# Attention on TensorE in steps of two heads instead of one, on one core of a two-block model

## What is computed

```
z = einsum('bhqd,bhkd->bhqk', qb, k) * scale            # qb: a block of 128 queries
# stick-breaking:
log_keep = where(past, log_sigmoid(-z), 0.0)
log_later = cumsum(log_keep, axis=3, reverse=True) - log_keep
w = where(past, exp(log_sigmoid(z) + log_later), 0.0)
o = einsum('bhqk,bhkd->bhqd', w, v)
# softmax (latent heads of 64 + 32 columns):
s = where(kpos <= qpos, z, neg);  p = softmax(s);  o = einsum('bhqk,bhkd->bhqd', p, v)
```

## Time and profile before

| | |
|---|---|
| median of 3 runs | 2439.66 us (2438.17 to 2441.11) |
| the profiled execution's own time | 2441.37 us |
| its span, first to last instruction | 2439.6 us |
| PE busy | 2364.3 us (97%) |
| DVE busy | 1379.0 us (57%) |
| ACT busy | 980.8 us (40%) |
| POOL busy | 241.9 us (10%) |

### The profile page before, as it was taken

One profiled execution on the slowest core, in us unless ns is written; L12 is line 12 of the kernel. 1 busy time (PEld: TensorE's weight loads), 2 busy tenths in 40 slices (PEclk: granted clock), 3 DMA queues, 4 the chain that ended last, 5 costly groups with the idle time before them and its releaser, 6 DMA issues.

```text
span 2439.6 us, 35763 instructions
## 1 busy us (share of the span) xinstructions
PE 2364.3 (97%) x13448; PEld 1887.9 (77%) x13448; DVE 1379.0 (57%) x1936; ACT 980.8 (40%) x1507; POOL 241.9 (10%) x192
## 2 busy tenths in 40 slices
PE   8999999999999999999999999999999999999998
PEld 6765777888887765777888887777888888788887
DVE  4557867666545447857656545675443445533443
ACT  5535435323235535535323244564332233422332
POOL 0041210000022032301000002101000001000001
PEclk9999999999999999999999998999999999999999
DMA  4210014656432211003656521222222232222322
GB/s 158 81 61 24 19 49 143 192 195 193 144 103 78 87 61 35 19 29 122 197 190 195 167 95 60 87 86 93 98 95 95 95 97 76 78 95 96 100 97 86
DMA packets 68796, 248.33 MB, mean 102 GB/s; under 512 B 7632, under 2 KB 8144, under 8 KB 68688
## 3 DMA queue, kind: packets, MB, share of 16 engines
q1 hardware_dynamic: 68688, 246.85, 30.8%
HBM read 244.72 MB, written 2.10 MB: 101 GB/s over the span
## 4 chain that ended last, share of the span: by engine, by line
PE 85%; DVE 7%; ACT 4%; issue 2%; DMA 0%; POOL 0%; SPq 0%; DVEq 0%; ACTq 0%
PE dense L588 24%; PE dense L590 24%; PE dense L589 24%; PE aux L695 2%; PE aux L882 1%; ACT wh L1352 1%; PE aux L852 1%; DVE wl L1966 1%; PE aux L869 1%; PE aux L960 1%; PE aux L971 1%; PE aux L1056 1%; PE aux L856 1%; PE dense L616 1%; PE aux L702 0%
## 5 line engine op out<-in xcount | busy, mean ns | idle before, releaser
L588 PE MATMUL dense<-xh,wh 128*128 128x512 f32 x1840 | 734.0, 399 | 25.4 <-DVE wl L1966 10.7
L1352 ACT ACTIVATE wh<-raw 128x1024 fp32r<-128x1024 f32 x346 | 366.7, 1060 | 944.0 <-PE dense L590 936.8
L1966 DVE TENSOR_TENSOR wl<-raw,wh 128x1024 fp32r<-128x1024 f32 x346 | 427.1, 1235 | 535.4 <-ACT wh L1352 533.9
L590 PE MATMUL dense<-xh,wl 128*128 128x512 f32 x1840 | 718.3, 390 | 0.0
L589 PE MATMUL dense<-xl,wh 128*128 128x512 f32 x1840 | 718.2, 390 | 0.0
L588 PEld LDWEIGHTS dense<-xh,wh 128*128 128x128 f32 x1840 | 346.6, 188 | 122.2 <-issue 28.0
L590 PEld LDWEIGHTS dense<-xh,wl 128*128 128x128 f32 x1840 | 346.4, 188 | 73.5
L589 PEld LDWEIGHTS dense<-xl,wh 128*128 128x128 f32 x1840 | 346.7, 188 | 73.0 <-issue 4.1
L588 PE MATMUL dense<-hidh,wh 128*128 128x512 f32 x928 | 363.5, 392 | 4.9 <-DVE hidl L1998 2.1
L589 PE MATMUL dense<-hidl,wh 128*128 128x512 f32 x928 | 361.9, 390 | 0.0
L590 PE MATMUL dense<-hidh,wl 128*128 128x512 f32 x928 | 361.7, 390 | 0.0
(11 more groups left out here) (386 smaller groups left out, 2432.6 us busy)
## 6 DMA issues: line engine op xcount, KB each, us to landing
raw<-stream SPq DMA_DIRECT2D x362, 512.0 KB, 3.4
mraw<-mod_stream SPq DMA_DIRECT2D x96, 512.0 KB, 4.2
x<-x_t SPq DMA_DIRECT2D x4, 512.0 KB, 7.2
y_t<-x SPq DMA_DIRECT2D x8, 256.0 KB, 2.0
cst<-consts SPq DMA_DIRECT2D x1, 993.0 KB, 9.3
band<-bands SPq DMA_DIRECT2D x1, 576.0 KB, 4.6
cond<-c_rows SPq DMA_DIRECT2D x1, 512.0 KB, 10.5
pv_next<-vecs SPq DMA_DIRECT2D x3, 82.5 KB, 4.6
```

Source lines behind the costliest of these rows:

```text
L588: pe.matmul(o, a, h, start=first, stop=False)
L590: return pe.matmul(o, b, h, start=False, stop=last)
L1352: act.activation(wh[:, slot].rearrange("p k m -> p (k m)"), raw[:, slot, :], ACT.Copy).then_inc(hi_done, 1)
L1966: tt(wl[:, slot].rearrange("p k m -> p (k m)"), raw[:, slot, :], wh[:, slot].rearrange("p k m -> p (k m)").bitcast(F32), SUB)\
```

## The change

PE's attention goes in 16 steps j of two units, 2j and 2j+1. A step is now: dense part of unit 2j; scores of both heads of step j+1, their two large matmuls next to each other and then the two masks; turn of unit 2j; values of step j-1, for each block of keys first head 0, then head 1; turn of unit 2j+1; dense part of unit 2j+1. `bonus` and `key_norm` follow the turn of their unit. The turned weights get a third place, and ACT's copy of unit u waits for the values of unit u-3. The order on DVE and ACT stays.

```diff
+        wT_slots = (wT[:, 0, :], wT[:, 1, :], at("wT_third", [P, S], wag_at + 2048)[:])
...
-                def scores(u):
-                    kind, pair, i, e = UNITS[u]
-                    n, q0, z = (i + 1) * P, i * P, zbank[u % 3]
-                    if u >= 3:
-                        pe.wait_ge(w_act, L * NU + u - 2)
...
+                def scores(j):
+
+                    kind, pair, i, _ = UNITS[2 * j]
+                    n, q0 = (i + 1) * P, i * P
+                    z = [zbank[(2 * j + e) % 3] for e in range(2)]
+                    if j >= 1:
+                        pe.wait_ge(w_act, L * NU + 2 * j - 1)
+                    for e in range(2):
+                        if kind == "sb":
+                            r = slice(64 * e, 64 * e + 64)
+                            pe.matmul(z[e][:, 0:n], sbq[r, pair, q0:q0 + P], sbk[r, pair, 0:n],
+                                      start=True, stop=False)
...
+                    for e in range(2):
+                        pe.matmul(z[e][:, q0:q0 + P], top_half(const("ident")), top_half(neg),
+                                  start=False, stop=True)\
+                          .then_inc(z_ready, 1)
...
-                def values(u):
-                    kind, pair, i, e = UNITS[u]
+                def values(j):
+                    kind, pair, i, _ = UNITS[2 * j]
                     q = (2 if kind == "mla" else 0) + pair
-                    pe.wait_ge(wT_ready, L * NU + u + 1)
-                    if i == 0 and e == 0 and q >= 2:
+                    pe.wait_ge(wT_ready, L * NU + 2 * j + 2)
+                    if i == 0 and q >= 2:
...
+                    for k in range(i + 1):
+                        for e in range(2):
+                            m = pe.matmul(aux[4 + q % 2][64 * e:64 * e + 64, i * P:(i + 1) * P],
+                                          v[:, k, 128 * pair + 64 * e:128 * pair + 64 * e + 64],
+                                          wT_slots[(2 * j + e) % 3][:, k * P:(k + 1) * P],
+                                          start=(k == 0), stop=(k == i), skip_group_check=True)
+                    m.then_inc(av_done, 2)
...
-                scores(1)
-                for u in range(NU):
+                for j in range(NU // 2):
+                    u = 2 * j
                     if u < SB_UNITS:
                         krv_part(u)
-                    if u == 0:
+                    if j == 0:
                         pe.wait_ge(lora_read, L * 12 + 12)
-                    if u + 2 < NU:
-                        scores(u + 2)
+                    if j + 1 < NU // 2:
+                        scores(j + 1)
                     turn(u)
-                    if u >= 1:
-                        values(u - 1)
...
-                values(NU - 1)
+                    others(u)
+                    if j >= 1:
+                        values(j - 1)
+                    turn(u + 1)
+                    others(u + 1)
+                    if u < SB_UNITS:
+                        krv_part(u + 1)
+                values(NU // 2 - 1)
...
-                    if u >= 2:
-                        act.wait_ge(av_done, L * NU + u - 1)
-                    act.activation(wT[:, u % 2, 0:n], aux[2][:, 0:n], ACT.Copy)\
+                    if u >= 3:
+                        act.wait_ge(av_done, L * NU + (u - 3) // 2 * 2 + 2)
+                    act.activation(wT_slots[u % 3][:, 0:n], aux[2][:, 0:n], ACT.Copy)\
                        .then_inc(wT_ready, 1)
```

More of the change, by code:

```diff
@@ L844, in attention @@
             def attention(L, pl):
-                def scores(u):
-                    kind, pair, i, e = UNITS[u]
-                    n, q0, z = (i + 1) * P, i * P, zbank[u % 3]
-                    if u >= 3:
-                        pe.wait_ge(w_act, L * NU + u - 2)
[L850 to L857, removed]
+                def scores(j):
[9 more added lines that the diff above has]
+                                      start=True, stop=False)
+                        else:
+                            h = 2 * pair + e
+                            pe.matmul(z[e][:, 0:n], qh[0:96, h, q0:q0 + P], kh[0:96, h, 0:n],
+                                      start=True, stop=False)
                     neg = const("neg_sb" if kind == "sb" else "neg_mla")
-                    pe.matmul(z[:, q0:q0 + P], top_half(const("ident")), top_half(neg),
-                              start=False, stop=True)\
-                      .then_inc(z_ready, 1)
+                    for e in range(2):
+                        pe.matmul(z[e][:, q0:q0 + P], top_half(const("ident")), top_half(neg),
+                                  start=False, stop=True)\
+                          .then_inc(z_ready, 1)
                 def turn(u):
@@ L918, in attention, with others @@
                 pe.wait_ge(up_act, L * 6 + 6)
-                scores(0)
-                scores(1)
-                for u in range(NU):
-                    if u < SB_UNITS:
-                        krv_part(u)
-                    if u == 0:
-                        pe.wait_ge(lora_read, L * 12 + 12)
-                    if u + 2 < NU:
-                        scores(u + 2)
-                    turn(u)
-                    if u >= 1:
-                        values(u - 1)
+                def others(u):
                     if u in BONUS_AT:
@@ L934, in attention @@
                         key_norm(KEYS_AT.index(u))
-                values(NU - 1)
+                scores(0)
+                for j in range(NU // 2):
+                    u = 2 * j
+                    if u < SB_UNITS:
+                        krv_part(u)
+                    if j == 0:
+                        pe.wait_ge(lora_read, L * 12 + 12)
+                    if j + 1 < NU // 2:
+                        scores(j + 1)
+                    turn(u)
+                    others(u)
[3 more added lines that the diff above has]
+                    others(u + 1)
+                    if u < SB_UNITS:
+                        krv_part(u + 1)
+                values(NU // 2 - 1)
             def prepare_chunks(L):
```

## The result

The changed kernel takes 2447.05 us (median of 10 runs, 2444.31 to 2451.33) where the kernel before, beside it, takes 2441.48 us (10 runs, 2438.17 to 2444.99): a ratio of 1.0024, 95% interval 1.0015 to 1.0034. It is slower by 5.6 us. The forecast was 2431.9 us, with a range from 2424 to 2443, so the time lies outside the range on the slower side. The profiled execution took 2450.43 us with a span of 2448.7 us, 9.1 us more than the span before.

A forecast was written before the change was run, and what follows sets the result against it. PE was taken to bound the stick-breaking stage, with PE and DVE both near full in the softmax units. Per layer 12.1 - 9.7 = 2.4 us plus 1.5 softmax gives 3.9, 7.8 for both: 2431.9 us, range 2424 to 2443.

The forecast's parts named there:

- Both overlaps: Stick-breaking units: two heads' scores and values each run twice as fast on PE, saving 5.9 and 4.5 us a layer.
- The dense entries: Dense share of the stick-breaking stage: 16 entries on PE become 9, saving 1.5 us a layer in fixed parts.
- The waits at the second turn: Stick-breaking steps: PE waits for DVE's weights or ACT's copy, sum 9.7 us a layer, 2.55 us in step 1.
- the 12.1 us taken off PE: PE's queue before unit 16, per layer: savings in scores, values, dense entries and second turns, less turning unit 15.
- The third place for turned weights: Frees ACT's copy from the values before last; ACT is idle there, so worth nothing by itself.
- what is added: PE waits at the second turn: Stick-breaking stage: DVE's order unchanged, less PE work ahead of second turns, so 9.7 us of waits a layer, uncovered.
- the wait of 1.29 us: Ahead of unit 16, kernel before: followed by a window at clock 1.00, cited against the low clock coming earlier.
- The softmax term: Softmax units: values fall by some 5.5 us but DVE limits next, so 1.5 us gained a layer.
- the third rival: Clock stays low among the softmax units as PE idles longer: 2458 us if it covers the stretch; 8%.
- Values don't overlap: Rival: scores overlap but products with values don't, most of that overlap only turning into waiting; 2434.9 us; 12%.
- nothing overlaps: Rival: neither scores nor values overlap, 1.7 us saved, 3.3 us of waits a layer; 2442.9 us; 12%.
- The waits stay away: Rival: ACT and DVE pulled ahead, so no second-turn waits and 13.6 us gained a layer; 2412.5 us; 6%.

The follow-up runs named there:

- e13: e1's order with neither overlap: each score followed by its own mask, the two heads' values on either side of the first turn; 2436.53 us, ratio 0.9984.
- e1: Changed kernel with the second head's dense part moved back ahead of that head's turn, both overlaps kept; 2420.62 us, ratio 0.9915.
- e7: e1 with the products with values head by head, all key blocks of head 0 and then all of head 1; 2421.69 us, ratio 0.9923.
- e10: e1 with head 0's products with values ahead of the first turn and head 1's behind it; 2428.74 us, ratio 0.9951.
- e2: Changed kernel with DVE making the second head's weights ahead of refill where a chunk ends in an even unit, PE untouched; 2427.31 us, ratio 0.9946.
- e4: Changed kernel with spare 128 x 512 matmuls ahead of the second turns of steps 1, 3, 4 and 7, output unchanged; 2442.11 us, ratio 1.0007.
- e14: e12 with the softmax pairs' values on either side of the first turn, only stick-breaking pairs keeping the overlap; 2416.65 us, ratio 0.9900.
- e11: Changed kernel's order with neither overlap: each score followed by its own mask, the heads' values on either side of the first turn; 2450.02 us, ratio 1.0038.
- e12: e1 with the dense part of unit 1 moved ahead of unit 0's turn too; 2415.35 us, ratio 0.9891.
- e8: e1 with each head's score directly followed by its mask, so the two large score matmuls are not neighbours; 2426.80 us, ratio 0.9936.

## Why the prediction was wrong

**What was right.**

- Both overlaps, a factor of two each, 5.9 + 4.5 = 10.4 us: 10.1 us, by e13 and e1. The factor was right; the sixteen records of the earlier trace rows that stood for "no overlap" had a wait for a copy in them (see e7), which did not matter for the price of 0.11 us a record.
- The Trainium skill ("TensorE: Matmul & The Clock Gate", Part 3) was cited with its rule on when a weight load overlaps matmuls in flight; from it the prediction took that the values would not overlap. The rows at 883.50 to 883.67, and e10 beside e1, show that they do.
- The dense entries, 1.5 us: by the starts of the records, the dense part of the stage went from 63.4 us to 66.4 in layer 0 and 64.7 in layer 1. Beside the same matmuls at the upper clock in other runs, the low clock cost 4.7 and 3.1 us of that, which leaves 1.8 us saved in both.
- The waits at the second turn, 9.7 us: 11.1 + 0.5 us now, less the 1.8 us that unit 0 waited before, is 9.8 in layer 1 (9.2 in layer 0). The single ones, forecast and measured in layer 1: step 1 2.55 and 2.52, step 4 1.5 and 1.7, step 6 1.25 and 0.8, step 7 1.85 and 2.0. e2 shows the cause that was named.
- Taken together: the stage was to fall by 2.4 us to 90.1. Without the low clock's share (4.7 and 3.1 us) it is 90.6 and 91.4 us, so 1.9 and 1.1 us of the 2.4 came. Since the waits were right, it is the 12.1 us taken off PE that were some 1 us too many: 11.0 came. In layer 1 the scores gave 5.6 for 5.9; the values 4.0 for 4.5, since the last product ahead of each waiting turn takes 0.27 us for 0.20; the turns nothing for 0.2; and 0.5 us of other matmuls now start inside the stage.
- The third place for turned weights was priced at nothing; no run takes it out alone, so that is not shown.

**The step that failed** is "what is added: PE waits at the second turn". It priced a wait at its own length, and the low clock in the stage at nothing. In the runs the waits of 2.5 and 2.0 us in steps 1 and 7 cost their length and then 1.6 us more each, since the dense matmuls behind them run for 3.4 us at 1.2 GHz; in layer 0 unit 0's wait does so too. That is 4.7 + 3.1 = 7.8 us for both layers, against 4.8 us that the sum gave as gain there. e4, which fills the waits of steps 1, 3, 4 and 7, gets 4.9 us back. The prediction weighed the low clock as a rival, but looked for it only among the softmax units, and took the wait of 1.29 us with a clock of 1.00 behind it as evidence against it. Neither that wait nor unit 0's 1.8 us has a low clock behind it in the kernel before, and there is no longer wait in its stages.

**The softmax term** (1.5 us a layer, bounds 0 and 3) was 1.2 us in layer 1 and -2.1 us in layer 0, where the low clock lasted 17.1 us for 6.8. This is the third rival in a small size and later than it was placed; 3.9 us of the miss are here. Over the 28 softmax stretches of the table the length goes with the time at the low clock: 42.3 to 42.9 us where that is 3.4 us or less, 42.0 to 45.0 where it is 6.8 to 10.7 us, 43.8 to 46.4 where it is 13.5 us or more. What makes the clock fall more in one kernel than in another e14 did not settle, and it stays open.

**The balance.** Forecast was -7.8 us; the clock in the stages puts 7.8 on top, the savings that fell short 1.8, the softmax units 3.9: +5.7, where the medians give +5.6. The terms come from one profiled execution of each kernel, whose spans differ by 9.1 us (it has the 2.3 and 1.4 us named above beside them), so that the sum meets the medians this closely is in part luck; the softmax term is the least certain.

**The rivals.** "Values don't overlap" and "nothing overlaps" had the wrong premise. For the second a price was given, 2442.9 us; e11 builds that case and takes 2450.02, for the reasons under e11: the price had the failed step in it as well. "The waits stay away", 2412.5 us at 6%, is what e12 is: 2415.35 us, once the order of PE is changed for it.

## What to carry to other kernels

Where two parts of one engine's queue wait for the same other engine, the work that lies between them is what hides that engine, so shortening the queue or moving that work changes a wait by as much as it saves: write down for each wait what lies ahead of it after the change. A wait inside a stretch of large matmuls may cost more than its length (here 1.6 us on top of 2.0 or 2.5), because the matmuls behind it can run at the lower clock; fill it, or move a block of dense work ahead of the waiting instruction (26 us here, by moving one call). Before calling an optimisation worthless, try it with the waits gone: in layer 1 the same two overlaps gave 3.7 us in one order and 10.1 in the other.

## What the runs showed of the hardware that was not expected

- **Two column halves run at once even when their matmuls aren't neighbours in the queue.** In e7 the second head's products start 0.006 us after the first head's fifth record, with three of the first head's eight still to come; sixteen records take 1.51 us, and 1.02 when the halves alternate. Eight records of one half alone take 1.02 us too, and with a turn over all columns between the halves the overlap is gone (e10).
- **The length of a wait alone does not tell whether the clock falls.** The stage of the kernel before has a clock of 1.00 with a wait of 1.8 us at unit 0 in it. The changed kernel waits 1.50 us at unit 0 in layer 0, with the low clock behind it, and 2.13 us in layer 1 without. In e11 a wait of 1.08 us, with turns and values around it, is followed by dense matmuls 0.43 us apart:

```profile
867.93 0.44 PE L873 MATMUL aux<-cst,wts 128*128 128x128 f32 x2
868.30 0.43 PE L886 MATMUL aux<-wT,vsb 128*64 128x128 f32 x2
869.81 0.60 PE L873 MATMUL aux<-cst,wts 128*128 128x128 f32 x2 [1.08 <-DVE wts L2197]
870.06 0.77 PE L589 MATMUL dense<-xh,wh 128*128 128x512 f32 x1
870.63 0.63 PE L590 MATMUL dense<-xl,wh 128*128 128x512 f32 x1
871.06 0.63 PE L591 MATMUL dense<-xh,wl 128*128 128x512 f32 x1
```

  What decides beside the length, these runs don't tell.
- **A small matmul costs more between other kinds.** From its start to the next, a mask of 128 x 128 takes 0.07 us ahead of a turn and 0.16 us ahead of a score (e8's rows at 909.98 and 908.76).
